# Layer 0's Strassen cycles: VectorE and GpSimd trade the low parts of T3 and T1

## What is computed

```python
def trunk(x, cond, ctx_ret, ctx_k, ctx_v, weights):
    ...
    for layer in range(DEPTH):
        m = jax.nn.silu(cond) @ ada_w[layer] + ada_b[layer]
        ...
        sh1, sc1, g1, sh2, sc2, g2 = (m[..., i, :] for i in range(6))
        ...
        h = rmsnorm(x, norm_g[layer, 1]) * (1 + sc2) + sh2
        x = x + g2 * (jnp.square(jax.nn.relu(h @ mlp_w1[layer])) @ mlp_w2[layer])
```

## Time and profile before

| | us |
|---|---|
| median of 3 runs | 1523.52 (1523.46 to 1523.79) |
| the profiled execution: device time | 1522.89 |
| the profiled execution: span of the trace | 1520.9 |
| PE busy in the span | 1499.2 (99%) |
| DVE busy | 1202.2 (79%) |
| ACT busy | 708.3 (47%) |
| POOL busy | 606.1 (40%) |
| one Strassen cycle of layer 0 (cycles 2 to 6) | 53.3 to 53.4 |

### The profile page before, as it was taken

How to read it: one execution, slowest core, us unless ns; L and a number is a source line. 1 busy time by engine, 2 the same in 40 slices (tenths; PEclk the granted TensorE clock), 3 DMA queues, 4 the chain that set the end, 5 groups by cost and what they waited for, 6 DMA issues and landing times. The chain is left out here.

```text
span 1520.9 us, 28265 instructions
## 1 busy us (share of the span) xinstructions
PE 1499.2 (99%) x11658; PEld 1463.4 (96%) x11658; DVE 1202.2 (79%) x1927; ACT 708.3 (47%) x1162; POOL 606.1 (40%) x386
## 2 busy tenths in 40 slices
PE   8999999999999999999999999999999999999998
PEld 7999999999999999999999999999999999999998
DVE  5448668666798878887897888774599999999996
ACT  5323333334444554455455434663454556545553
POOL 0133223214223666665675253101333564446531
PEclk9999999999999999999999999999999999999999
DMA  9455235213243335334435122001222222322222
GB/s 327 161 180 171 91 99 171 74 40 121 84 135 116 125 125 178 125 129 152 139 126 178 36 70 73 32 2 42 69 71 72 83 82 70 111 84 70 83 85 83
DMA packets 121119, 162.18 MB, mean 107 GB/s; under 512 B 4640, under 2 KB 83488, under 8 KB 120992
## 3 DMA queue, kind: packets, MB, share of 16 engines
q1 hardware_dynamic: 119760, 159.34, 32.3%
q10 hardware_dynamic: 1232, 1.05, 0.2%
HBM read 156.44 MB, written 3.93 MB: 105 GB/s over the span
## 5 line engine op out<-in xcount | busy, mean ns | idle before, releaser
L2051 POOL TENSOR_TENSOR wL<-raw,wH 128x512 fp32r<-128x512 f32 x180 | 290.7, 1640 | 631.6 <-ACT wH L1475 426.5
L1180 PE MATMUL ps<-fx,wH 128*128 128x320 f32 x1344 | 297.9, 310 | 0.1
L1180 PEld LDWEIGHTS ps<-fx,wH 128*128 128x128 f32 x1344 | 223.9, 188 | 3.2 <-issue 2.6
L1180 PE MATMUL ps<-fx,wL 128*128 128x320 f32 x672 | 207.7, 309 | 0.0
L2051 POOL TENSOR_TENSOR wL<-raw_high,wH 128x512 fp32r<-128x512 f32 x92 | 138.2, 1527 | 151.6 <-ACT wH L1475 143.1
L756 PE MATMUL ps<-hH,wH 128*128 128x320 f32 x576 | 181.3, 315 | 1.5 <-DVE hL L2137 0.9
L756 PE MATMUL ps<-hH,wL 128*128 128x320 f32 x576 | 178.0, 309 | 0.0
L756 PE MATMUL ps<-hL,wH 128*128 128x320 f32 x576 | 178.0, 309 | 0.0
L756 PE MATMUL ps<-wH,hH 128*128 128x256 f32 x560 | 162.1, 289 | 2.4 <-DVE hL L2137 2.1
L756 PE MATMUL ps<-wL,hH 128*128 128x256 f32 x560 | 158.4, 283 | 0.0
L756 PE MATMUL ps<-wH,hL 128*128 128x256 f32 x560 | 158.3, 283 | 0.0
(11 more groups left out here) (305 smaller groups left out, 3841.6 us busy)
## 6 DMA issues: line engine op xcount, KB each, us to landing
ada<-in_ada_w SPq DMA_DIRECT2D x40, 1024.0 KB, 6.0
raw<-in_mlp_w SPq DMA_DIRECT2D x64, 512.0 KB, 3.7
raw_high<-in_mlp_w SPq DMA_DIRECT2D x64, 512.0 KB, 3.8
raw<-in_even_w_in SPq DMA_DIRECT2D x28, 512.0 KB, 6.0
pre_w<-in_ada_w SPq DMA_DIRECT2D x16, 512.0 KB, 9.0
raw<-in_odd_w_qkv SPq DMA_DIRECT2D x10, 512.0 KB, 3.6
raw<-in_even_w_out SPq DMA_DIRECT2D x8, 512.0 KB, 3.6
raw<-in_odd_w_o SPq DMA_DIRECT2D x6, 512.0 KB, 3.6
```

The costliest lines, as they stand in the source:

```text
L1180: last = nc.tensor.matmul(ps[:, bank, 0:HALF], a_, b_, start=(opens and k == 0 and p_ == 0), stop=(k == nk - 1 and p_ == 2), skip_group_ch ...
L2051: last = nc.gpsimd.tensor_tensor(wL[:, at % 4, cs], source(key)[:, cs], wH[:, at % 4, cs].bitcast(F32), ALU.subtract)
```

## The change

In layer 0, DVE now makes the low part of T3 at the head of the cycle, where it made that of T1, and POOL that of T1 behind that of T2, where it made that of T3. Layer 1 stays as it is.

```diff
-P_DVE = ((T1, B22, B21, T4), (T2, T3, T1, B22, B21, T4))
+P_DVE = ((T3, B22, B21, T4), (T2, T3, T1, B22, B21, T4))
...
                 def strassen_cycle(c):
...
-                    t_lo(s, T1)
+                    t_lo(s, T1 if layer else T3)
                     if c == PLAIN:
                         s_low(4, 4)
...
                     held_out(0)
-                    t_lo(s, T1)
+                    t_lo(s, T1 if layer else T3)
                     held_out(1)
```

## The result

The changed kernel takes 1528.68 us, the median of 6 runs (1526.94 to 1530.99), beside 1523.56 for the kernel before on the same chip (6 runs, 1523.0 to 1524.26). The ratio is 1.0037, with a 95% interval of 1.0027 to 1.0047: 5.1 us slower. I forecast 1526.5, slower by 3.0, with a range of 1521.2 to 1530.5. The direction holds and the time lies in the range, but 2 us of the 5 were not in the sum, and the experiments show that the sum was put together wrongly: one term was missing, and another has about the right size by luck.

A forecast was written before the change was run, and what follows sets the result against it. PE was taken to set the time, with 2.2 us of waits on POOL's low parts to win back. The sum -2.2 + 2.6 + 2.6 = +3.0 on 1523.5 gave 1526.5 us, range 1521.2 to 1530.5.

The forecast's parts named there:

- The gain, 2.2 us: Layer 0, cycles 2 to 6: PE's wait for T3's low part from POOL goes away, 0.44 us per cycle.
- DVE's instructions around it keep their places and lengths: POOL's T1 low part: takes what T3's took, ending at 591.74 in cycle 3, with 3.3 us of slack.
- The cost in SP's queue: Load of q T1 issued 3.47 us later, with `ada_w` and q B22 behind it: 2.6 us lost in cycles 4 and 6 each.
- I keep the 7.8 after the later issue too: Cycle 3: q B22 still lands 7.8 us after q T1's issue, at 599.6; cycles 2, 3 and 5 cost nothing.
- the edge of 8.1: Rival, cycles 2, 3, 5: q B22 landing over 8.1 us after q T1's issue costs 1.35 us each; chance 0.22.
- The slow ones as before: Cycles 4 and 6: `ada_w` again takes 8.4 and 8.3 us, and PE loses 2.6 us in each.
- More like their place than like chance: Slow `ada_w` loads of cycles 4 and 6 come in neighbouring pairs, so they were expected to come again.
- on-time loads: Rival: long `ada_w` loads of cycles 4 and 6 don't recur; 1521.3 us, or 1523.9 with one; chance 0.17.
- The clock: Rival: after 2 us PE waits in cycles 4 and 6 the clock falls, 1.2 us each, 1528.9; chance 0.07.

The follow-up runs named there:

- Experiment 3: The change with DVE's T3 low part waiting for ACT's T1 high part, and `ada_w` issued ahead of q T1: 1521.14 us, ratio 0.9986.
- experiment 2: The change with the `ada_w` block issued ahead of the load of q T1 instead of behind it: 1523.88 us, ratio 1.0005.
- experiment 5: The kernel before, with q T1's load issued only when POOL's low part of T3 is done: 1528.12 us, ratio 1.0032.
- the second ones: The change run once more, nothing altered, beside the kernel before: 1529.9 us, ratio 1.0044.
- exp. 1: The change, with DVE starting T3's low part only when ACT has made T1's high part: 1526.82 us, ratio 1.0026.
- Experiments 1 to 6: The sixth: the change, but DVE makes both T3's and T1's low parts and POOL neither; 1523.88 us, ratio 1.0004.
- experiment 4: The kernel before, with the `ada_w` block issued ahead of q T1 and nothing else: 1523.19 us, ratio 1.0000.

## Why the prediction was partly right

**The gain, 2.2 us: right.** Experiment 3 has it (1523.24 - 1521.14 = 2.1 by the medians, 2.2 in the trace). In the change itself the waits at T3 are gone too, but the next point takes the time.

**"DVE's instructions around it keep their places and lengths": this step failed.** I used it for T1 on POOL, and let T2 end where it did (587.19 in cycle 3). The place in the order was kept, but neither the start nor the length. DVE's old instruction could not begin before ACT's 532.68. I had read this as no wait, since the row shows no idle time: it was a few hundredths, and they decided who of DVE and POOL goes first. In the rows, whoever starts first runs its plain 1.21 or 1.29 us, and the other takes about 2.3. The rule of the Trainium skill that the forecast cites (SBUF — State Buffer, SBUF: two separate sides) says the same: the two lock each other out for a whole instruction, and the one that starts first has the lock. I had used it for POOL's lengths, and had not asked who starts first after the change. The price is the difference of experiments 2 and 3, 1523.88 - 1521.14 = 2.7 us. With it the gain is gone, and about 0.6 more.

**The cost in SP's queue: right in kind**, and shown alone by experiment 5. There it costs 1528.12 - 1523.06 = 5.1 us. In the change it costs 5.1 less the 0.6 by which experiment 2 lies above its kernel before (1523.88 - 1523.24), so 4.5 us by the first runs of the change, and 6.8 - 0.6 = 6.2 by the second ones. I had 5.2. The size is about right, but the cycles are not those of the forecast, so that it is right is luck:

| cycle | issue of q T1 to landing of q B22, forecast | the change | again | exp. 1 | exp. 5 |
|---|---|---|---|---|---|
| 2 | 7.8 | 7.7 | 7.8 | 7.7 | 7.8 |
| 3 | 7.8 | 8.8 | 8.7 | 8.6 | 8.7 |
| 4 | 10.15 | 7.9 | 7.8 | 7.6 | 8.1 |
| 5 | 7.7 | 8.8 | 7.6 | 8.6 | 8.8 |
| 6 | 9.9 | 9.7 | 10.4 | 8.2 | 8.2 |

"I keep the 7.8 after the later issue too" holds in cycle 2. In cycle 3 it is 8.6 to 8.8 each time, beyond the edge of 8.1, and PE loses 1.3 us behind the burst in the change, where I had 1.35. "The slow ones as before" fails in cycle 4: `ada_w` took 6.2 us there, and the 2.6 us that I had booked did not come. In cycle 6 it took 8.1 and 8.7, and PE lost 3.0 us in the change (1.52 up to the burst, 1.48 behind it) where I had 2.6. "More like their place than like chance" was wrong for cycle 4. It held for cycle 6 in both profiles of the change, but not in experiment 5, where that block took 5.9. Behind the second burst the profiled execution of the change lost 0.50, 1.33, 0.66, 1.32 and 1.48 us in cycles 2 to 6, and of these places only the last was in the sum as it came. So two rivals, on-time loads in cycle 4 and the edge in cycles 3 and 5, each came true for a part, and their errors go against each other.

**Waits in the second matrix: not in the sum.** In cycles 2 and 4 PE was 0.40 and 0.59 us late at a product of the second matrix. (The row's number in brackets, 0.24, is less, since a matmul's row is 0.31 long where the next one normally starts after 0.15.) PE's wait is put down to issue. DVE's row before it, and POOL's, in cycle 2:

```profile
560.52 1.46 DVE L2631 TENSOR_TENSOR fx<-u,fx 128x640 fp32r<-128x640 f32 x1
...
558.33 2.97 POOL L2051 TENSOR_TENSOR wL<-t_first,wH 128x512 fp32r<-128x512 f32 x2 [2.22 <-ACT wH L1493]
...
562.08 0.39 PE L1180 MATMUL ps<-fx,wH 128*128 128x320 f32 x1 [0.24 <-issue]
```

DVE's operand `fx` takes 1.46 us where it took 0.81 at 559.73 before. POOL's pair ends at 561.30, while before it had ended at 559.77, as `fx` began. PE's matmul follows the end of `fx`, 561.98. I had followed the late loads to the next wait of PE, and no further: cycles 2 and 4, which I took to be free or to pay at the m = 1 group, pay here. That the q B22 load is behind this too is shown by experiments 2 and 3, where the waits are gone. That it is POOL's lock that lengthens `fx` is read from the rows, and was not tried by itself.

**The clock: not in the first profile, once in the second.** In the first, the granted clock is 1.00, the 2.4 GHz level, from cycle 2 to cycle 6, with PE's idle times of 1.02 and 1.17 us among them. In the second it fell to 0.50, the 1.2 GHz level, behind the idle time of 1.93 us before the burst of cycle 6, at the price of 1.2 us that the rival had named for each such wait. The rival needed two waits of 2 us and had one. Experiments 1 to 6 have no idle time of PE over 1.1 us in this stretch, and no fall. How many of the unprofiled runs of the change had one is not known.

**The sum as it should have been**: -2.1 for the gain (1521.14 - 1523.24), +2.7 for T2, and +5.1 for the loads by experiment 5, which is +5.7. The change measured +5.1 and, the second time, +6.8, on either side of it. Without the T2 waits the late loads cost 1526.82 - 1521.14 = 5.7, beside the 4.5 or 6.2 above, so these medians do not show whether the two terms add up. My sum had +3.0: the T2 term is what was missing.

**Open**: why the change takes 5.1 us in one set of runs and 6.8 in the other (the fall of the clock is 1.2 of it in the one profile that has it), and why cycle 3's q B22 takes 1 us more than cycle 2's. The bytes moved in slices of 0.25 us, from SP's issue of q T1 on, first cycle 2 and then cycle 3:

```profile
GB/s 0 0 0 0 82 66 238 254 385 360 418 393 393 410 426 377 410 377 385 434 418 402 418 410 393 393 336 164 49 0 0 0 0 0 66 0 0 0 0 0
```

```profile
GB/s 0 0 0 0 98 98 197 303 377 410 385 393 442 401 410 377 385 401 418 401 426 418 442 369 377 377 270 115 66 16 25 25 25 8 0 0 0 0 0 33
```

The rate is about the same up to 6.75 us. Then cycle 3 has a thin tail of some packets until 8.5 us, and the load is landed at 8.8. What holds those packets up I do not know.

## What to carry to other kernels

A late load is cheap where it is needed late; what counts is what stands behind it in its queue. Before a buffer's release is moved, ask which loads behind it need no such buffer, and put them ahead: here that alone turned +5.1 us into +0.6. And where two engines lock each other out, as DVE and POOL do here, a wait of a few hundredths of a microsecond can be what orders them, so an instruction that becomes free of a wait has to be placed anew against the other engine, above all where PE reads what the other one makes.

## What the runs showed of the hardware that I had not expected

- A difference of 0.06 us in DVE's start moved about 1.1 us from DVE to POOL (POOL's T2 3.51 to 4.57, DVE's low part 2.31 to 1.21). It did so in each of five cycles, in both profiles of the change.
- The slow `ada_w` loads that the forecast used had a slow issue as well. SP took 0.93 and 0.94 us to issue those of cycles 4 and 6 before, which then took 8.4 and 8.3 to land, and 0.96 and 1.04 for that of cycle 6 in the two profiles of the change (8.1 and 8.7 us). The usual issue takes 0.47 and the landing 5.9 to 7.1 in cycles 2 to 6. It does not work the other way round: in experiment 1 an `ada_w` block issued in 0.89 us landed after 6.0, and in experiment 4 a load of q T1 issued in 1.86 us landed after 6.5.
- The `ada_w` blocks before these, issued at 626.9 and 733.7 in the kernel before, had a slow issue in every trace of this case (0.58 to 1.38 us), so that part is the place. Whether they are slow to land (6.0 to 8.8 us), and whether the next block is slow too, changes between kernels and partly between runs of one kernel.
- A single idle time of PE of 1.93 us, and a burst of small matmuls behind it, came before a fall of the granted clock to 0.50 (second profile of the change, 1.2 us lost). Behind idle times of up to 1.17 us in the first profile it stayed at 1.00.
